# Earlier picks, places refilled in halves, packed S5 matrices and wide expert rows in a four-layer kernel

## The reference

```python
for layer in range(DEPTH):                     # even, odd
    mix = even_mixer(...) or odd_mixer(...)    # ends with  concat(heads, other) @ w_out
    x = x + mix
    h = rms_norm_2(x, norm_ffn_g[layer])
    x = x + hier_moe(h, ...)                   # 32 experts: (silu(h @ w_gate) * (h @ w_up)) @ w_down

# s5_mixer: per group of 16 channels a diagonal complex state of 64
lam_bar = exp(lam * step);  b_bar = (lam_bar - 1) / lam * (b_re + i b_im)
y = Re(c_mat @ states) + d_skip * u
```

## Time and profile before

| what | us | note |
|---|---|---|
| median of three runs | 1538.08 | 1537.22 to 1539.68 |
| the profiled execution | 1537.3 | its span is 1535.4; 1.9 lie around it |
| PE (matmul) busy | 1292.0 | 84% of the span |
| PE weight loads | 698.4 | beside the matmuls |
| DVE busy | 462.7 | 30% |
| ACT busy | 278.2 | 18% |
| POOL busy | 266.0 | 17% |
| DMA | | 498.18 MB, mean 324 GB/s |

### The profile page before, as it was taken

The page is one execution under the profiler, slowest core; times in us unless marked ns, Lnnn a source line. Parts: engine busy times, 40 slices in busy tenths (PEclk is TensorE's granted clock), DMA queues, the critical chain, the costliest instruction groups (busy, mean ns, idle before and its releaser), DMA issues. The chain is left out here.

```text
span 1535.4 us, 21931 instructions
## 1 busy us (share of the span) xinstructions
PE 1292.0 (84%) x9264; PEld 698.4 (45%) x9264; DVE 462.7 (30%) x903; ACT 278.2 (18%) x547; POOL 266.0 (17%) x158
## 2 busy tenths in 40 slices
PE   9999999999999999667767667999998776676666
PEld 5754466547878554223223322755544232232232
DVE  2554662654845531111000101286311010010011
ACT  2042410423322210300000000115211101011011
POOL 0676226641000008790000000000000000000000
PEclk9999999999999999888889999999999888999999
DMA  9932452336430699999999999946799999999997
GB/s 371 359 127 82 182 227 84 140 138 271 183 139 31 255 416 423 428 432 433 428 433 426 436 429 427 394 166 241 275 424 431 428 435 430 427 434 430 427 436 300
DMA packets 36514, 498.18 MB, mean 324 GB/s; under 512 B 5728, under 2 KB 8544, under 8 KB 12256
## 3 DMA queue, kind: packets, MB, share of 16 engines
q1 hardware_dynamic: 36448, 497.22, 77.9%
HBM read 495.11 MB, written 2.10 MB: 324 GB/s over the span
## 5 line engine op out<-in xcount | busy, mean ns | idle before, releaser
L3190 PE MATMUL banks<-weight_ring,spare_weights_arena 128*32 128x512 f32 x1472 | 220.9, 751 | 143.9 <-DMA weight_ring<-in_moe_weights 142.4
L3111 DVE TENSOR_TENSOR spare_weights_arena<-spare_weights_arena,banks 64x512 f32<-64x512 f32 x32 | 22.1, 690 | 658.5 <-ACT spare_weights_arena L3030 658.5
L3190 PEld LDWEIGHTS banks<-weight_ring,spare_weights_arena 128*32 128x32 f32 x1472 | 56.4, 132 | 297.5 <-issue 244.6
L3157 PE MATMUL banks<-spare_weights_arena,x 128*128 128x64 f32 x960 | 110.8, 274 | 0.0
L3157 PEld LDWEIGHTS banks<-spare_weights_arena,x 128*128 128x128 f32 x960 | 109.9, 192 | 0.0
L3030 ACT ACTIVATE spare_weights_arena<-banks 64x512 f32<-64x512 f32 x32 | 18.9, 591 | 501.8 <-PE banks L3190 501.8
L3204 PE MATMUL banks<-weight_ring,spare_weights_arena 128*32 128x512 f32 x728 | 89.4, 624 | 13.9 <-issue 7.6
L1001 POOL TENSOR_TENSOR weight_ring<-spare_weights_arena,weight_ring 128x2048 f32<-128x2048 f32 x16 | 74.0, 4638 | 70.9 <-DVE spare_weights_arena L845 38.5
L1114 PE MATMUL banks<-weight_ring,x_normed_hT_mix 128*128 128x512 f32 x192 | 84.7, 592 | 0.0
L3238 PE MATMUL banks<-spare_weights_arena 64*128 64x512 f32 x240 | 59.6, 615 | 20.9 <-ACT spare_weights_arena L3036 20.9
L338 PE MATMUL banks<-weight_ring,x_normed_hT_mix 128*128 128x512 f32 x128 | 56.3, 595 | 0.0
(11 more groups left out here) (557 smaller groups left out, 1823.7 us busy)
## 6 DMA issues: line engine op xcount, KB each, us to landing
weight_ring<-in_moe_weights SPq DMA_DIRECT2D x42, 4096.0 KB, 26.9
weight_ring<-in_moe_weights SPq DMA_DIRECT2D x53, 2048.0 KB, 19.0
weight_ring<-in_ring_weights SPq DMA_DIRECT2D x35, 2048.0 KB, 12.2
spare_weights_arena<-in_moe_weights SPq DMA_DIRECT2D x21, 2048.0 KB, 51.5
x_normed_hT_mix<-in_moe_weights SPq DMA_DIRECT2D x16, 2048.0 KB, 54.8
spare_weights_arena<-in_moe_weights SPq DMA_DIRECT2D x7, 4096.0 KB, 54.5
weight_ring<-in_ring_weights SPq DMA_DIRECT2D x4, 1024.0 KB, 6.0
x_normed_hT_mix<-in_moe_weights SPq DMA_DIRECT2D x4, 1024.0 KB, 4.9
```

The lines of the kernel that those rows point to most:

```text
L3111: dve.tensor_tensor(hid[0:2 * CAP, :], sil[0:2 * CAP, :], b_gu[2 * CAP:4 * CAP, :], ALU.mult).then_inc(s_h, 1)
L3157: ins = pe.matmul((b_x, b_dn)[k // 4][:, k % 4 * 2 * CAP:(k % 4 + 1) * 2 * CAP], g.x[:, tt, k * P:(k + 1) * P], Pr[:, tt, :], start=(tt == ...
L3190: ins = pe.matmul(b_gu[q:q + CAP, :], xg[:, 2 * quarter + k, e * CAP:(e + 1) * CAP], up_w(where, quarter, e)[:, which, k, :], start=(quart ...
```

## The change

- **Picks.** Pair 0's gather starts after tile 0 is picked (`gather_halves`); DVE copies the first quarter before winners and the second before shares; the differences move behind the pick; two idle matmuls that keep PE's clock go.
- **Output weights by rows.** The two `w_out` chunks are K rows 512 to 1023 and 0 to 511, each with all columns. The first is free after the first four `out_part` calls; place 3 is loaded then, half of pair 1's place 3 after the transposes, place 4 in two halves after banks 2 and 3.
- **Packed S5 matrices.** `s5_bc` (768 KB, one DMA, ahead of pair 3) replaces the three matrices; POOL expands it with a mask. The rows of parameters go: `odd_par` shrinks from 2780 to 862 columns (431 KB), the causal mask is made by POOL, and lambda is brought into rows by 32 small PE matmuls after pair 2 (`spread_rows`) and two ACT copies. ACT's constants move from after pair 3 to after pair 1.
- **32 KB rows.** Odd pairs are loaded as three 4 MiB loads too, but for each layer's last pair, whose places 2 to 5 stay alone. The last odd pair's loads move behind the loop over turns; SP reads a second turn count.

```diff
         sp.wait_ge(s_mix, TT)
         sp.dma_start(moe_params(g), A["moe_par"][0]).then_inc(g.moe_par_landed, 16)
         router.part_of(sp, 4, 0, extra[3][0])
-        sp.wait_ge(s_w, 3)
+        sp.wait_ge(s_w, 1)
         weights(0, 3, ring[3], first)
+        sp.wait_ge(s_mt, TT)
+        router.part_of(sp, 3, 0, extra[2][0])
         sp.wait_ge(s_w, 4)
-        weights(0, 4, ring[4], first)
-        weights(1, 3, extra[2][0], second)
+        first_half(0)
+        sp.wait_ge(s_w, 5)
+        first_half(1)
+        router.part_of(sp, 3, 1, extra[2][1])
...
-            w = g.chunk(pe, c0 + 5 + ch)
+            w = g.chunk(pe, c0 + (5 if ks[0] == 4 else 6))
             for kt in ks:
-                ins = pe.matmul(ps[j], g.mixT[:, kt, tt * P:(tt + 1) * P], w[:, kt, :], start=(kt == 4), stop=(kt == 3))
+                ins = pe.matmul(ps[j], g.mixT[:, kt, tt * P:(tt + 1) * P], w[:, 4 * ch + kt % 4, :],
+                                start=(kt == 4), stop=(kt == 3))
...
+        pool.wait_ge(s_pw, 4)
+        TT(col["lr"], col["rho"], col["cs"], ALU.mult).then_inc(v.s_lam, 1)
+        TT(col["li"], col["rho"], col["sn"], ALU.mult).then_inc(v.s_lam, 1)
...
-        def load_later(bank, pair, n, more):
+        def load_later(bank, pair, n, more, apart=()):
 
             for d in range(SLOTS // 2):
-                if 2 * d in alone[bank]:
+                if 2 * d in apart:
                     for j in (2 * d, 2 * d + 1):
                         released(j, n, more)
                         load(later[bank], bank, pair, j)
...
+            released(2, 0, 2)
+            sp.dma_start(g.s5.packed, A["s5_bc"]).then_inc(g.s5_bc_landed, 16)
             for j in range(SLOTS):
...
-                if j == 0:
-                    for dst, name in ((g.s5.B[:, 0], "s5_b"), (g.s5.C[0], "s5_c"), (g.s5.bT, "s5_bT")):
-                        sp.dma_start(dst, A[name]).then_inc(g.s5_bc_landed, 16)
...
-            with sp.Fori(0, NP // 2 - 2) as i:
+            with sp.Fori(0, NP // 2 - 3) as i:
                 for bank in range(2):
                     load_later(bank, i * 2 + (4 + bank), t * NP + i * 2, 5 + bank - lag)
+            load_later(0, NP - 2, t * NP, NP - 1 - lag)
             with sp.If(t < T - 1):
+                load_later(1, NP - 1, t * NP, NP - lag)
                 for pair in range(4):
                     load_later(pair % 2, pair, t * NP, NP + pair + 1 - lag)
+        load_later(1, NP - 1, more_turns * NP, NP - lag, apart=alone)
...
         pick_first()
+        gathered_first((0,))
+        router.winners_of(dve)
         router.largest(dve)
+        gathered_first((1,))
         router.shares(dve)
-        gathered_first()
+        gathered_first((2, 3))
         router.gates(dve)
+        dve.wait_ge(s_eq, 1)
...
+        def gather_halves():
+            pe.wait_ge(g.dve_steps.sem, router.tile_0_picked)
+            for quarter in range(2):
+                for k in range(2):
+                    of_quarter(quarter, 0, k)
+            pe.wait_ge(s_pm, 1)
+            for quarter in range(2):
+                of_quarter(quarter, 1, 0)
+                of_quarter(quarter, 1, 1).then_inc((s_G0, s_G)[quarter], 1)
...
+        def spread_rows():
+            v = g.s5
+            pe.wait_ge(v.s_lam, 2)
+            for name, bank in (("lr", b_x), ("li", b_dn)):
+                for a in range(HT):
+                    for i in range(4):
+                        q = 4 * i + a
+                        ins = pe.matmul(bank[32 * i:32 * i + 32, a * P:(a + 1) * P], v.col[name][:, q:q + 1].to_broadcast([P, 32]),
+                                        ident, start=True, stop=True, tile_position=(0, 32 * i))
+                ins.then_inc(v.s_row, 1)
+            pe.wait_ge(v.s_pw, 6)
...
-        gather_first(0)
-        gather_first(1)
+        gather_halves()
         of_pair(0, first, 0, None, opens=True)
         of_pair(1, second, 1, None)
         of_pair(2, third, 2, None)
+        if ly == 0:
+            spread_rows()
```

More of the change, by code:

```diff
@@ L3193, in gate_up, with down @@
             ins.then_inc(s_gu, 1)
[L3195 removed]
+        def down(half, where, bank, rounds, last=False):
             if rounds is None:
                 arrived_early(bank, 4 + half)
+            elif last:
+                arrived_last(4 + half, rounds)
             else:
```

202 lines of the change are left out of this document (118 added, 84 removed).

## The result

The changed kernel took 1527.38 us, the median of six runs (1525.37 to 1528.39), beside 1537.69 us for the kernel before (six runs, 1534.91 to 1539.68): a ratio of 0.9930, 95% interval 0.9917 to 0.9943. It is faster by 0.7%; 1525.3 us was forecast, with 1521 to 1531 as the range. The profiled execution took 1527.14 us (span 1525.2, before 1535.4), so of the 12.8 us of the sum 10.2 came.

What follows compares the result with a forecast made beforehand. The weight stream of the two expert layers, at about 430 GB/s, was taken as the bound. Terms of 6.4 + 1.6 + 2.9 + 1.9 = 12.8 us off the 1538.08 us median gave 1525.3 us, range 1521 to 1531.

Steps and rivals of the forecast that it cites:

- Pick: Pick and first gather, both expert layers: first gate matmul and releases of pairs 0 and 1 come 1.6 us earlier.
- Head of the first layer: Weight stream up to pair 3's last place, first expert layer: 6.4 us gained, 1.6 of it from the earlier pick.
- Place 1 (issue 580.2) follows without a hole: Pair 3, first expert layer: place 1's load joins place 0's without a break, leaving the stream 6.9 us ahead.
- The two wide bounds, 5 and 7: Limits in us on the first expert layer's 6.4 us gain; 5 assumed a cold start at each edge.
- Wide odd pairs: 32 KB rows in eleven odd pairs: 0.32 us saved for each, 1.6 us in the first layer, 1.9 in the second.
- Rival (a): Wide rows give nothing; the 0.32 us comes from something else in an odd pair: 9.3 us gained, 1528.8; chance 0.12.
- Rival (d): Each separate DMA pays a 1.6 us cold start even when queued: 35 us instead of 3.5, 1493.8; chance 0.01.
- Head of the second layer: Start of the second expert layer's stream: 2.9 us gained, 1.6 from the pick, 1.3 from nothing left queued.
- Which is a cold start anyway and stays: Second expert layer, 1108.78 to 1117 us: the 1.6 us lost at 345 GB/s would remain after the change.
- The added wait: PE's row spreading after pair 2, first expert layer: 2.8 us, covered by queued loads with 0.1 to spare, priced 0.
- rival (c): PE waits at the spreading for POOL's lambda, resuming at 628 instead of 601: 14 us slower, 1552; chance 0.03.
- rival (e): An edge of the first layer breaks and half its head start is lost, 3 us: 1528.3; chance 0.12.

Runs made afterwards that it cites:

- The filled edge: Changed kernel with the packed S5 matrices (0.75 MiB) fetched a second time between place 0 and place 1 of pair 3, first expert layer: 1531.23 us.
- the early packed load: Changed kernel with the packed S5 matrices fetched ahead of the first expert layer, right behind the odd parameters, into columns free from the start: 1531.15 us.

## Why the prediction was right, and where it was wrong

**Pick:** right. Ranks to pair 0 went from 6.15 to 4.55 us in both layers, and the release with it.

**Head of the first layer:** the step that failed. 6.4 us was forecast; to pair 4 it is 3.33 (89.45 - 86.12). The sentence that fell is "Place 1 (issue 580.2) follows without a hole". I gave a load 1.6 us from its issue and took it as covered when the queue still had 2 us of work. Place 1, issued at 580.00, landed at 591.27, 7.23 us after place 0 (584.04), where a place takes 4.90 in the stream. Of the 2.33 us lost, the first of its sixteen parts shows 0.8, beside the hole of 221 and 385 GB/s. The other 1.5 is that the last part fell further behind the first, from 1.93 to 3.43 us; an instruction packet had started at 587.6. Place 0, whose windows show 362 GB/s, had lost only 0.15 us. In whole, 574 to 588 us ran at 407 GB/s in the kernel before, with its 1.5 MiB behind place 0, and at 375 in the changed one:

```profile
574.00:588.00 14.00, 13.30 (x115) 4.78 (x108) 0.57 (x2) 1.43 (x3) 8.83 (x17) 1.00 0.99 407
...
574.00:588.00 14.00, 13.30 (x115) 5.87 (x108) 1.12 (x2) 6.24 (x11) 9.65 (x20) 1.00 0.98 375
```

That is 1.8 us less than full rate. At pair 4's first load the last part comes 3.44 us behind the first, in the kernel before 1.90. PE waits for the last, so 1.5 of the 3.1 missing us are this distance. The stream had also ended pair 2 late: its last place landed at 577.13, and the forecast's 574.6 and 0.8 give 575.4. It ran from 545 to 574 us at 423 GB/s and not at 430, and restarted slowly at 541. A part of the bytes that were saved was thus spent at the edges that their absence opened. The two wide bounds, 5 and 7, were too narrow because both took the same cold start. The filled edge and the early packed load show the hole from either side. How much of the last part's distance comes from the restart and how much from the instruction packet stays open.

**Wide odd pairs:** the mechanism is right, the size is half: 0.16 us and not 0.32 for a pair, 1.8 us and not 3.5. The 0.32 was read from PE's starts (29.07 and 29.39 us apart), and 0.17 of it is the alternation of PE's start behind its wait; the landings of the kernel before are 29.15 and 29.30 us apart. Rival (a) had the right doubt and half of the right size. Rival (d) is out: two more DMAs cost at most 0.08 us each. The Trainium skill ("DMA: Bandwidth & Descriptors", "Anatomy of one DMA") has a fit of about 2 us for each DMA, stated for transfers that GpSimd issues; it doesn't give the price of one more of SyncE's DMAs in a full queue.

**Head of the second layer:** 2.9 forecast, 4.8 found. "Which is a cold start anyway and stays" was wrong: the 1.6 us that were lost after 1108.78 came from a release that arrived 1.3 us before the end of the queue, and pair 2's place 0 landed 7.12 us after the load ahead of it in place of 4.90. Now the release comes on an empty queue, and the load lands at 1109.98, 7.26 us after its issue, which is the cold start as forecast (1.6 + 4.9 + 0.8); from 1108 on the stream runs at 436 GB/s. A second loss of the kernel before was seen by no term: pair 3's first load, issued at 1132.76 with some 10 us of work ahead of it, landed 11.26 us after the load before it, where 9.7 is usual. That is no dry queue; an instruction packet had started at 1149.4. At pair 15 the last part is 4.49 us behind in the kernel before and 2.08 in the changed one. This is 2.4 of the 4.8 us, and the 2.4 that are left are a little less than the forecast.

**The added wait:** priced at 0, and 0 is right. The margin is 1.3 to 2.0 us, not 0.1. That PE resumed at 600.12 and not later than 601.0 is luck: the spreading and the wait behind it (1.95 and 1.87 us) add 3.8 us and not 2.8, but the row that I counted from, 599.78, had 1.7 us of a stretch at 0.5 in it (592 us, pair 2). POOL's second product of lambda, which PE waits for, in the changed kernel's trace:

```profile
583.04 0.22 POOL L2153 TENSOR_TENSOR spare_weights_arena<-spare_weights_arena 128x16 f32<-128x16 f32 x1
```

PE's spreading began at 596.3, so rival (c) never came near.

**Sum:** the first head 3.1 us short, the wide rows 1.7 short, the second head 1.9 over, and 0.2 from ahead of the ranks: 12.8 - 3.1 - 1.7 + 1.9 + 0.2 = 10.1, against 10.2. The total was close partly by luck: of the two heads one lost and one gained by the same two things, which no term held, the edge of a nearly dry queue and the distance of the last part. That about half of the first head was lost is what rival (e) described, but I gave it 0.12 and no mechanism.

## What to carry to other kernels

A stream of weights can lose time wherever its queue runs nearly dry, and it can do so even when the next load is asked for 1 to 2 us before the queue is empty. So count, at each release, how many microseconds of transfer are queued: a release with some 2.9 us queued lost nothing here, and 0.75 MiB put into such a gap cost 0.6 to 1.3 us instead of 1.8. When several edits feed the same queue, price them together, since undoing one of two gave 1.6 and 2.3 us where both gave 4.8. Read when the last part of a load lands, and not only how many bytes moved: two kernels at 430 GB/s differed by 1.4 and 2.4 us in that alone, and an alternation of PE's starts was taken for one of the loads. And compare stages from a common landmark, not totals, before an effect of 1 us is believed.

## What the runs showed of the hardware that I had not expected

The granted clock of TensorE fell to 0.5 for 3 to 10 us in stages where PE is busy nearly throughout, in some executions and not in others of almost the same code, with the same busy time ahead (2.63 and 2.64 of 3 us). At the ranks such a stretch costs 4.3 us up to pair 2 (47.7 against 43.45), near 572 us it costs 1.7 up to pair 2 and, with the packed matrices ahead of place 0, next to nothing at pair 4 (86.32 and 86.12), since the stream is the limit there.

A restart after the queue was empty (172 and 254 GB/s, then no second hole) left pair 4 0.4 to 1.1 us earlier than one that began just before it emptied (362, then 221 and 385 at the next load).

The sixteen parts of a load need not land together, and a distance that has once opened stays: 3.43 us at 591 us and 3.48 at 941 in the changed kernel, while the rate is 430 GB/s throughout. Of 47 growths by more than 0.4 us, 43 followed a packet of the instruction queue, in full queues too (1.5 us with some 10 us queued).
